# Attention's products between the two groups of products of a half slot

## The reference, cut to what matters

```
proj = rmsnorm(x) @ w_in              # first block: q, k, v of 16 heads, three gates
x = x + (gates * attentions @ w_branch) @ w_out
x = x + (silu(conv(u_gate)) * conv(u_val)) @ w_ffn_down
for l in range(2):                    # second block
    x = layernorm(ALPHA * x + 0.5 * swiglu(x))
    qa, ka, va, zb, xbc, dtb, qc, kc, vc, gpre = split(x @ w_mix_in[l])
    o_a = diff_attention(qa, ka, va); o_b = mamba2(zb, xbc, dtb); o_c = stick_breaking(qc, kc, vc)
    x = layernorm(ALPHA * x + sum(sigmoid(gpre) * (o @ w_branch)) @ w_out)
    x = layernorm(ALPHA * x + 0.5 * swiglu(x))
```

## Time and profile before

| | us |
|---|---|
| median of 3 runs | 2034.75 |
| lowest, highest | 2033.75, 2035.18 |
| the profiled execution | 2032.28 |
| its span | 2030.5 |

### The profile page before, as it was taken

The page is one execution under the profiler, slowest core; times in us unless marked ns, Lnnn a source line. Parts: engine busy times, 40 slices in busy tenths (PEclk is TensorE's granted clock), DMA queues, the critical chain, the costliest instruction groups (busy, mean ns, idle before and its releaser), DMA issues.

```text
span 2030.5 us, 35295 instructions
## 1 busy us (share of the span) xinstructions
PE 2002.8 (99%) x14178; PEld 1826.7 (90%) x14178; DVE 1392.0 (69%) x2079; ACT 1095.3 (54%) x1761; POOL 146.5 (7%) x150
## 2 busy tenths in 40 slices
PE   8999999999999999999999999999999999999998
PEld 6889899899988889998999989998888989899996
DVE  7866688745556777678775556556578677886555
ACT  6677466534443667658544443433468756753442
POOL 1200000000000001720000000000000380000000
PEclk9999999999999999999999999999999999999999
DMA  7434456545754444553645754575344554464563
GB/s 276 161 126 145 156 187 211 203 137 187 254 174 147 166 144 142 187 171 125 228 134 187 249 176 146 186 254 185 131 166 142 161 184 155 146 208 146 186 208 123
DMA packets 273003, 355.23 MB, mean 175 GB/s; under 512 B 10203, under 2 KB 226029, under 8 KB 272877
## 3 DMA queue, kind: packets, MB, share of 16 engines
q1 hardware_dynamic: 271533, 349.23, 51.2%
q0 software_dynamic: 1344, 4.23, 0.8%
HBM read 352.35 MB, written 1.08 MB: 174 GB/s over the span
## 4 chain that ended last, share of the span: by engine, by line
PE 89%; DVE 6%; ACT 3%; issue 2%; POOL 1%; DMA 0%; DVEq 0%; ACTq 0%; POOLq 0%
PE ps L798 24%; PE ps L800 17%; PE ps L807 17%; PE ps L808 7%; PE ps L802 7%; PE ps L792 4%; PE ps L794 4%; PE ps L793 4%; DVE ring_r L1881 2%; PE ps L1277 1%; PE ps L1023 1%; POOL small L2630 1%; ACT ring_hi L1400 1%; PE ps L1208 1%; DVE conv_s L2376 1%
## 5 line engine op out<-in xcount | busy, mean ns | idle before, releaser
L1881 DVE TENSOR_TENSOR ring_r<-ring,ring_hi 128x1024 fp32r<-128x1024 f32 x602 | 732.6, 1224 | 417.7 <-ACT ring_hi L1400 416.4
L1400 ACT ACTIVATE ring_hi<-ring 128x1024 fp32r<-128x1024 f32 x602 | 632.6, 1059 | 595.1 <-PE ps L807 364.6
L798 PE MATMUL ps<-xT_hi,ring_hi 128*128 128x256 f32 x2784 | 682.2, 284 | 1.7 <-issue 1.7
L800 PE MATMUL ps<-xT_r,ring_hi 128*128 128x256 f32 x2784 | 672.5, 280 | 0.0
L798 PEld LDWEIGHTS ps<-xT_hi,ring_hi 128*128 128x128 f32 x2784 | 524.7, 188 | 16.8 <-issue 12.1
L800 PEld LDWEIGHTS ps<-xT_r,ring_hi 128*128 128x128 f32 x2784 | 524.8, 189 | 0.0
L807 PE MATMUL ps<-xT_hi,ring_r 128*128 128x256 f32 x2784 | 384.9, 280 | 0.0
L807 PEld LDWEIGHTS ps<-xT_hi,ring_r 128*128 128x128 f32 x2784 | 353.1, 188 | 0.0
L2630 POOL TENSOR_TENSOR small<-small,const 128x1 f32<-128x1 f32 (+3 forms) x32 | 38.0, 1187 | 1841.5 <-DVE small L2305 1268.5
L802 PE MATMUL ps<-ring_hi,tok_r 128*128 128x512 f32 x344 | 135.7, 395 | 0.0
L798 PE MATMUL ps<-ring_hi,xT_hi 128*128 128x512 f32 x312 | 125.4, 402 | 2.6 <-issue 2.6
(11 more groups left out here) (374 smaller groups left out, 2881.8 us busy)
## 6 DMA issues: line engine op xcount, KB each, us to landing
ring<-in_w_mix_in SPq DMA_DIRECT2D x88, 1024.0 KB, 5.0
ring<-in_ffn_w_in SPq DMA_DIRECT2D x80, 1024.0 KB, 5.0
ring<-in_ffn_w_out SPq DMA_DIRECT2D x44, 1024.0 KB, 4.8
ring<-in_w_branch SPq DMA_DIRECT2D x24, 1024.0 KB, 5.1
ring<-in_w_in SPq DMA_DIRECT2D x22, 1024.0 KB, 5.0
ring<-in_w_ffn_up SPq DMA_DIRECT2D x22, 1024.0 KB, 5.0
ring<-in_w_ffn_down SPq DMA_DIRECT2D x11, 1024.0 KB, 4.9
ring<-in_w_mix_out SPq DMA_DIRECT2D x8, 1024.0 KB, 5.9
```

Of the source, the lines that this page charges most:

```text
L798: pe.matmul(out_, stat[0], mov[0], start=first, stop=False)
L800: pe.matmul(out_, stat[0], mov[1], start=False, stop=False)
L1400: act.activation(half_of(high_of(s), s, q), half_of(ring[:, s % SLOTS, :], s, q), ACT.Copy).then_inc(w_hi, 1)
L1881: return dve.tensor_tensor(lo, whole, hi.bitcast(F32), ALU.subtract)
```

## The change

`half` no longer does its low group itself. It does the high group and returns a function, `low_group`, which waits for the low part, does the low group and releases the half slot. The two loops over the steps, of the first block and of a layer, call that function at the next "half" step, before that half's own waits, and once more after the last step. So what TensorE does between two halves (the beat, and `conv_rows`, `memory`, `dt_rows`, `dt` and the like) now stands between a half's high group and its low group. The order of ScalarE, VectorE, GpSimd and SyncE is not touched, nor any operand. `out_rows` calls the function at once, and `features`, used in the feed-forward part, is split in two functions and keeps its order.

```diff
                 for q in range(HALVES):
-                    half(L, c0, 0, q)
+                    half(L, c0, 0, q)()
...
                         high_products(bank(2 * c.pair + t), ..., h == 0 and k == 0)
-                    wait_block(L, s, q)
-                    for t, k in places:
-                        mov = [v[:, k, :] for v in w]
-                        mm = low_product(bank(2 * c.pair + t), ..., h == 1 and k == 3)
+                    def low_group():
+                        wait_block(L, s, q)
+                        for t, k in places:
+                            mov = [v[:, k, :] for v in w]
+                            mm = low_product(bank(2 * c.pair + t), ..., h == 1 and k == 3)
+                        used(mm, q)
                 else:
-                    mm = features(tiles(2 * c.pair + h)[:, q, :], block(s, TOK), act, q, lambda: wait_block(L, s, q))
-                used(mm, q)
+                    out_, w = tiles(2 * c.pair + h)[:, q, :], block(s, TOK)
+                    features_high(out_, w, act, q)
+                    def low_group():
+                        wait_block(L, s, q)
+                        used(features_low(out_, w, act, q), q)
+                return low_group
...
+            low_group = nothing
             for step in steps1:
                 if step[0] == "half":
+                    low_group()
                     if step[1].act == "memT" and step[2:] == (0, 0):
                         wait_xT(1)
-                    half(None, *step[1:])
+                    low_group = half(None, *step[1:]) or nothing
...
+            low_group()
             pe.wait_ge(in_loaded, 16)
...
                 for step in mixed[L]:
                     if step[0] == "half":
+                        low_group()
...
-                        half(L, *step[1:])
+                        low_group = half(L, *step[1:]) or nothing
...
+                low_group()
                 out_rows(L, out2, 4 * (L + 1), lambda: turn_tile(norm_event(L, 1), x, 0))
```

More of the change, by code:

```diff
@@ L892, in half, with features_high @@
                         high_products(bank(2 * c.pair + t), [a[:, 4 * h + k, t * P:(t + 1) * P] for a in act], mov, mov, h == 0 and k == 0)
-                    wait_block(L, s, q)
-                    for t, k in places:
-                        mov = [v[:, k, :] for v in w]
-                        mm = low_product(bank(2 * c.pair + t), [a[:, 4 * h + k, t * P:(t + 1) * P] for a in act], mov, mov, h == 1 and k == 3)
-                else:
-                    mm = features(tiles(2 * c.pair + h)[:, q, :], block(s, TOK), act, q, lambda: wait_block(L, s, q))
-                used(mm, q)
-            def features(out_, w, act, q, wait_low):
+                    def low_group():
+                        wait_block(L, s, q)
+                        for t, k in places:
+                            mov = [v[:, k, :] for v in w]
+                            mm = low_product(bank(2 * c.pair + t), [a[:, 4 * h + k, t * P:(t + 1) * P] for a in act], mov, mov, h == 1 and k == 3)
+                        used(mm, q)
+                else:
+                    out_, w = tiles(2 * c.pair + h)[:, q, :], block(s, TOK)
[4 more added lines that the diff above has]
+                return low_group
+            def features_high(out_, w, act, q):
                 for k in range(KD):
@@ L905, in features, with features_low @@
                     high_products(out_, stat, [a[:, k, :] for a in act], stat, k == 0)
-                wait_low()
+            def features_low(out_, w, act, q):
                 for k in range(KD):
@@ L910, in features, with nothing @@
                 return mm
+            def features(out_, w, act, q, wait_low):
+                features_high(out_, w, act, q)
+                wait_low()
+                return features_low(out_, w, act, q)
+            def nothing():
+                return None
             def up(f, it, js, event=None, midway=None):
```

## The result

| | before | changed |
|---|---|---|
| median, us | 2033.08 (8 runs) | 2040.37 (8 runs) |
| lowest, highest | 2029.19, 2035.18 | 2039.20, 2043.45 |
| the profiled execution | 2032.28 | 2043.39 |
| its span | 2030.5 | 2041.6 |

The ratio is 1.0039, 95% interval 1.0029 to 1.0049: 7.9 us slower (5.9 to 10.0; the two medians differ by 7.3), where 6.1 were forecast. The profiled execution is one of the slower ones of the changed kernel, so its span is 11.1 us longer than that of before. Lines after 798 to 808 have moved: 1054 is now 1076, 1219 is 1244, 1234 is 1259, 1327 is 1352, 1400 is 1428.

What follows compares the result with a forecast made beforehand. TensorE, busy 2002.8 of 2030.5 us, was taken as the bound. Terms of 0.93 + 2 x 0.94 + 3.3 = 6.1 us on 2034.75 gave 2040.8 us, 0.30% slower, range 2033.8 to 2046 (the forecast's own 2038.8 to 2043.5).

Steps and rivals of the forecast that it cites:

- Low groups never wait: TensorE's idle time before low products is 0.0 in both modes, so the wait the new order would cover is empty.
- Cost 1, block 1: First block: TensorE reaches `pair1`'s wait for VectorE's norm earlier and waits longer, with the low group still to do; 0.93 us.
- Cost 1 in the layers: Each layer's `dscore` and `dout`: TensorE reaches waits fixed by other engines' queues earlier and waits longer; 0.94 us, twice.
- cost 2: ScalarE's split waits for a release now given one low group after the beat, delaying its queue; 1.65 us a layer, twice 3.3.
- Cost 2, differential attention: Exponentials come up to 1 us later, but their product is asked for only two halves on; counted 0.
- Cost 2, the rest: Later splits per layer: `turn_xs` 0.35 us, `snorm` to `ksum` 1.0, last `kout` 0.3; `sdecay` and `sout` 0.
- The sum: Whole kernel: 0.93 + 2 x 0.94 + 3.3 = 6.1 us slower, 2040.8 us, 0.30%; chance 0.43.
- Rival (e): TensorE's clock falls behind `pair1`'s wait, grown from 2.2 to 3.1 us; 1.7 us more, 2042.5; chance 0.04.
- (a): Only the longer waits cost, as ScalarE's and VectorE's queues have room; 2.8 us slower, 2037.6; chance 0.25.
- (b): Nothing moves: awaited chains start with the beats that feed them and all shifts together; 2034.75 us; chance 0.11.
- (c): Faster: earlier beats shrink waits in the stick-breaking loop; the layers' 4.6 us vanish, 2030.2; chance 0.07.
- (d): ScalarE becomes the bound of the softmax beats, losing 0.4 us a half, 19 at most; 2050; chance 0.10.

Runs made afterwards that it cites:

- early_after: The changed kernel, with the last high product of each half slot telling ScalarE that the high part's room is free; 0.9996 of the kernel before.
- late_before: The kernel before in its old order, with each half slot's release in the layers given late, in the middle of the next high group; 1.0052, 10.6 us slower.
- block1_only: The kernel before with the new order in block 1 alone and the old order in the layers; 1.0007, 1.4 us slower.
- cost1_away: New order in the layers only, except third xbc and first gate chunks, whose low groups are issued at once; 1.0026 of the kernel before, 5.3 us slower.
- early_before: The kernel before in its old order, with the high part's room released early to ScalarE; 0.9989, 2.2 us faster.
- early_layers: The kernel before with the early release of the high part's room and the new order in the layers alone; 0.9987, 2.6 us faster.

## Why the prediction came out, step by step

**Low groups never wait.** Right: 0.0 in both modes, before and after.

**Cost 1, block 1** (0.93). Right: the wait is 0.9 longer, `pair1` at the same time. With the wait filled and the clock at 1.00, block 1 loses 0.87 behind 72 us.

**Cost 1 in the layers** (0.94 each). The number was near (1.15 and a joint of 0.14), the reason was wrong, and this is the step that failed: "Both are late since ScalarE and VectorE still drain the third `xbc` chunk, whose products are released before the beat in either order." The products are; but the drain stands in ScalarE's queue behind a split, and the split behind the low group. early_after has the beats as early as the change and loses nothing there; late_before has them as late as before and loses 1.14. There is one mechanism in the layers, not two: cost 2.

**Cost 2, differential attention** (0). Wrong for the same reason. I had seen that the copy of 735.87 "had waited anyway" and would start up to 0.9 later, and compared that with ScalarE's mean slack over 70 us; the beats around the drain of `xbc` have none. The two errors cancel, since I had booked the 0.94 in the line above: that the layers' sum came out is, to that extent, luck.

**Cost 2, the rest.** `turn_xs` 0.35, measured 0.37. `snorm` to `ksum` 1.0, measured 1.07. The last `kout` 0.3, measured 0.10 and 0.20 in the two layers, 0.2 and 0.3 without the joint. `sdecay` and `sout` 0, measured -0.09, a joint. Following a split from the beat's end by 0.94 and 0.26, and then each engine's queue row by row, held to a tenth of a microsecond wherever I did it.

**The sum.** Forecast 6.1. By the profiles the layers cost 5.5 (forecast 5.2), block 1 between 2.3 and 3.5 (forecast 0.93); the timed runs give block 1 less, 1.4 to 3.2. The term that was mis-sized is block 1's, by the clock.

**Rival (e), the clock.** Given a chance of 0.04, with a price of 1.7; it came. Behind a wait of 3.1 us the clock fell in all four profiles that had one (the change twice, early_after, block1_only), and cost 1.4 to 2.6 there, beside the 0.9 of the wait. Behind the old wait of 2.2 us it fell in two of eight (cost1_away, early_before), at 1.5 each, so the kernel before pays it now and then too, and the change pays the difference. I had read one profile with 1.00 behind a wait of 2.2 us as a property of the kernel. The Trainium skill, "TensorE: Matmul & The Clock Gate", section "The HAM clock gate (the "warmup" mystery)", has the number of slow matmuls at a kernel's start vary from run to run of one kernel. The profiles here show the same for places inside it: the granted clock from 84 to 88 us was 0.55 in one execution of the change and 0.80 in another.

**Rivals (a) to (d).** (a) had the mechanism the wrong way round: it is cost 2 that the layers pay. (b), that the awaited chains move with their beats, is true of every chain in the layers, as early_layers shows, and only ScalarE's split hid it. (c) didn't occur: what the loop waits for is not the beat's start. (d) didn't: the waits of `dout` and `dscore` come once in each layer.

**Open.** Why the clock falls behind one and the same wait in one execution and not in the next; and the clock's share in the timed runs, which only the profiles show directly.

## What to carry to other kernels

Before moving work on the busiest engine, find which semaphore the moved work raises, which in-order queue waits on it, and what stands behind that wait; the moved instruction may cost nothing where it stands and everything where it signals. Give each buffer's release at the last instruction that reads that buffer, not at the end of the group it belongs to: it made this kernel 2.2 us faster and, in the layers, the order of its groups indifferent. A chain looks as if it had a time of its own until the queue that carries it is followed back to the last thing that it waited for.

## What the runs showed of the hardware that I had not expected

- The same wait leaves the clock alone in one execution and halves it in another (two of eight at 2.2 us, four of four at 3.1 us, none of two where products filled most of it; at `dout` in cost1_away, two of four at 1.6 us). The fall near 240 us, which the earlier trace rows show for the kernel before, is of the same kind: behind the same wait of 1.7 us the granted clock over 238 to 248 us was 0.83 in seven of the fourteen profiles, the kernel before and the change among them, and 1.00 in the other seven, among them the second profile of the change. Those without it are 1.4 to 1.5 us further on behind it. One profile doesn't settle whether a kernel is clear of it.
- A loop that no edit touches (first feed-forward part, ten turns from high group to high group) took 113.9 us in twelve profiles, 112.6 in one and 115.2 in one, and both kernels of the odd ones came back with 113.9. A difference of 0.13 us a turn over a loop is no effect of an edit until a second profile shows it.
